# A Mamba-style mixer step: decay exponents from broadcast running sums instead of matmuls, and x and B transposed into banks 4 and 5

## The chip, the cores and the metric

The kernel runs on one core of a Trainium2 chip (trn2). The metric is the device time of one execution in microseconds. Three runs of the kernel before took 2757.2, 2757.87 and 2758.27 us; the median is 2757.87.

## What is computed

One decoder layer over 2048 tokens of 1024 channels, behind 16 learned meta tokens, all in fp32:

```python
hn = rms_norm(h, norm_mix_w);  proj = hn @ w_in            # u | z | xBC | dt
y  = concat(pool_mixer(u), ssd_mixer(z, xBC, dt))          # 512 + 1536 channels
h  = h + y @ w_out
h  = h + relu(rms_norm(h, norm_ffn_w) @ w_ff1)**2 @ w_ff2
out = rms_norm(h, norm_f_w)
```

The change is in the SSD mixer. It works in chunks of 128 tokens, on 4 groups of 6 heads. With `a_cs` the running sum of dt times a over a chunk:

```python
seg    = a_cs[l] - a_cs[s]                       # exponent, l: reading token, s: source token
decay  = exp(where(l >= s, seg, -inf))
y_diag = ((C[l] . B[s]) * decay) @ (x * dt)
```

`a` is negative, so the exponent is at most 0 wherever l >= s.

## The kernel before, in words

The 2048 tokens are worked in 4 blocks of 512, each of 4 chunks. Every large fp32 product is made of three products of rounded parts (high x high, high x low, low x high). A block goes through "items": a group's five conv units (B, C and three tiles of x) and its z (three units in block 0, four pieces by chunk in blocks 1 to 3), then four pool items, then 16 units of the output product. A unit is 24 matmuls of 128x512 (`up_unit`, L1692), a z piece 24 of 128x384 (L1716), and the output product L1736. In block 0 the weights are split on the way: ScalarE makes the high part (`high_part`, L500), GpSimd the low part (`low_part`, L508), SyncE stores both to DRAM (L705), and the later blocks load them back. ScalarE's high part of item N waits for the store of item N-2, since both use the same slot. After the four blocks the feed-forward part follows (L1996, L2028), which the change doesn't touch.

The mixer has 16 steps a block (`mixer_plan`): step q is group g, chunk c. The order on each engine is written out by hand. On TensorE a step is: `unit(n1)` (none in the last four steps), `slot3(q-1)`, `slot1(q)`, one to three units n2, `y_offset(q)`, `y_transposes(q-1)`. So the mixer's small matmuls stand between units of the next group, which cover what the other engines do in the meantime; the last four steps have one pool unit each.

`slot1` makes the exponents of 6 heads x 128 columns with matmuls: L1783 multiplies `seg_s` (selectors and the negated running sums of the group) with `seg_l` (running sums spread over the heads, and the head selectors), two matmuls of 128x384 into banks 4 and 5; in block 0 L1778 first puts -1e30 below the diagonal. It then transposes x and B (L1794) into bank 2 and, in block 0, z (L1803) into bank 3, and makes C.B in bank 3 (L1805). Bank 2 is used for the transposes of y too (`y_transposes`, L1817), which is why `slot1` waits for `yT_lo`, the low part of y (`y_low`, L2271). `slot3` is the product inside the chunk (L1829) and the new state (L1836); `y_offset` (L1811) reads the state.

ScalarE, in each step: evacuates n1 (`evac`), applies tanh, makes E from the exponents (block 0: one Exp, L1379; later: Relu with scale -1 from PSUM, L1382, and Exp, L1385, which clamps in place of the mask), spreads the negated sums once a group (L1318, L1322), copies x (L1394) and z (L1399), squares y (L1313), scales y by its root (`y_norm`, L1306, root on GpSimd, L983 and L984), evacuates n2, and takes the high part of y (`y_high`, L1299). VectorE: `y_finish` (the sum L2243 and the y product with the gate, L2245), the conv taps (`taps`, L2165), the state sum (L2262), the triangle mask on C.B (L2345, not in block 0), E times C.B (L2347), x times dt (L2351, L2353), `finish` of items (L2195, or the pool chain L2202 to L2219 for pool items), yo (L2363), and `y_low`.

The running totals of a block: softplus on VectorE (`softplus_rest`, L455 to L465, in three parts at items 2, 3 and 4), the totals by two matmuls (`running_totals`, L1841 and L1843: inside unit 7 in block 0, after item 6 later), copies by VectorE at the last item (L2312 to L2315), transposes of the totals on TensorE (L1904).

Of the kernel before, what the change touches and what calls it, by code (L numbers as in the profile page):

```python
# [6 lines left out]
P = 128  # L7
# [7 lines left out]
FAR = -1e30  # L15
# [6 lines left out]
TB = 512  # L22
# [138 lines left out]
def build(nc, x, meta, norm_mix_w, w_in, pool_w, pool_scale, conv_w, conv_b, dt_bias, a_log,  # L161
          d_skip, ssm_norm_w, w_out, norm_ffn_w, w_ff1, w_ff2, norm_f_w, out):
    ctx = ExitStack()
    with ctx:
# [49 lines left out]
        ident_r = sb("ident_r", [P, P], F32R)  # L214
        barred = sb("barred", [P, P], F32R)
# [4 lines left out]
        acsT = win_tmp[0:56, 0:TB].bitcast(F32R)  # L220
        head_of = sb("head_of", [56, 8])
        in_group = sb("in_group", [56, 4])
        not_group = sb("not_group", [56, 4])
        seg_l = sb("seg_l", [120, CH, HEADS_PER_GROUP, P], F32R)
        seg_s = sb("seg_s", [120, 2, TB], F32R)
# [5 lines left out]
        v, nv, ev, s_, q_, dA, acs, alast = [steps_of[:, i * NB:(i + 1) * NB] for i in range(8)]  # L231
# [48 lines left out]
        hn_scr = nc.dram_tensor("hn_scr", [3, 2, P, 4, TB], F32).ap()  # L280
        T_scr = nc.dram_tensor("T_scr", [2, 4, 7, P, 4, TB], F32).ap()
# [61 lines left out]
        acsT_hi_ready = sig("acsT_hi_ready", 1)  # L343
        acsT_lo_ready = sig("acsT_lo_ready", 1)
        seg_l_ready = sig("seg_l_ready", CH)
        seg_s_ready = sig("seg_s_ready", GROUPS)
        xb_ps = sig("xb_ps", STEPS)
        ab_ps = sig("ab_ps", STEPS)
# [3 lines left out]
        fall_ready = sig("fall_ready", STEPS)  # L352
        zs_ready = sig("zs_ready", STEPS)
# [51 lines left out]
        p_x = [sem(f"p_x{t}") for t in range(CH)]  # L405
# [4 lines left out]
        pick = acc[0:56, 0, 0:HEADS]  # L410
# [14 lines left out]
        below = F[:, 5956:6084]  # L425
# [218 lines left out]
        with nc.Block() as block:  # L644

            @block.sync
            def _(sp):
# [40 lines left out]
                initial = [s for s in signals if s.start and s not in (state_ready, up_out)]  # L688
# [258 lines left out]
            def _(pool):  # L947
# [8 lines left out]
                pool.affine_select(out=below[:, :], in_=ones[:, :], compare_op=ALU.is_gt,  # L956
                                   fill=0.0, base=0, pattern=[[-1, P]], channel_multiplier=1)
# [206 lines left out]
            def _(act):  # L1164
# [152 lines left out]
                def negated_sums(b, g):  # L1317
                    nc.scalar.activation(seg_s[0:56, g % 2, :],  # L1318
                                         ones[0:56, :].unsqueeze(1).to_broadcast([56, CH, P]),
                                         ACT.Copy, scale=in_group[:, g:g + 1])  # L1320
                    acsT_lo_ready.wait(act, b, 1)
                    nc.scalar.activation(seg_s[64:120, g % 2, :], acsT[:, :].bitcast(F32), ACT.Copy,  # L1322
                                         scale=not_group[:, g:g + 1]
                                         ).then_inc(seg_s_ready.sem, 1)

# [10 lines left out]
                for b in range(BLOCKS):  # L1336
# [7 lines left out]
                    for n in range(ITEMS_G if b else UNITS_G):  # L1344
# [11 lines left out]
                        if n == (ITEMS_G if b else UNITS_G) - 1:  # L1356
# [4 lines left out]
                                                 ).then_inc(gains_ready.sem, 1)  # L1361
                    pending = None
                    for q, g, c, n1, n2 in mixer_plan(b):
                        if q == 0:
                            acsT_ps.wait(act, b, 1)
                            nc.scalar.activation(acsT[0:HEADS, :], bank[3][0:HEADS, :], ACT.Copy
                                                 ).then_inc(acsT_hi_ready.sem, 1)
# [1213 lines left out]
```

## Time and profile before

| what | value |
|---|---|
| median of 3 runs | 2757.87 us |
| the profiled execution | 2759.15 us, its span 2757.4 us |
| TensorE busy | 2733.2 us, 99% |
| VectorE, ScalarE, GpSimd busy | 58%, 43%, 40% |
| DMA | 505.75 MB, 183 GB/s in the mean |
| mean granted TensorE clock | 0.998 |

The span runs from the first to the last instruction; the time of the execution also holds what lies around it. "Busy" on TensorE counts the modelled, overlapping spans of matmuls: one of 128x512 is shown with some 390 ns, while 24 in a row take 5.47 us. What a matmul costs on the path is therefore read from the chain of waits, not from its own duration.

### The profile page before, as it was taken

What the parts mean: (1) busy time and instruction counts of PE and PEld (TensorE: products, weight loads), DVE (VectorE), ACT (ScalarE), POOL (GpSimd) and SP (SyncE); (2) the same over time, 40 slices, a digit from 0 to 9 for tenths busy, and PEclk for the clock granted to TensorE, in tenths of its full rate; (3) what the DMA queues carried; (4) which work ended last, traced back from release to release, by engine and by line L of the source; (5) the groups of instructions that cost most, each with busy time, mean ns of one, the idle gap of its engine ahead of it and who ended that gap; (6) DMA issues with size and microseconds to landing.
All of it is one profiled execution on the core that took longest, in us unless ns stands there. A gap on an engine that the chain in (4) does not pass through costs nothing.

```text
span 2757.4 us, 37228 instructions
## 1 busy us (share of the span) xinstructions
PE 2733.2 (99%) x14110; PEld 2260.5 (82%) x14110; DVE 1604.2 (58%) x2236; ACT 1182.4 (43%) x2110; POOL 1096.3 (40%) x799
## 2 busy tenths in 40 slices
PE   8999999999999999999999999999999999999998
PEld 6788778888788887888888888888888888888887
DVE  4687623666426665157663466664445666666666
ACT  2465544455325554155542645555445322222223
POOL 1365541223101222003223587855555435353434
PEclk9999999999999999999999999999999999999999
DMA  9766486443556335554336446674444942333323
GB/s 291 243 220 200 154 294 240 183 170 137 185 196 229 123 134 189 198 211 170 138 134 248 172 158 240 221 279 168 148 146 163 352 153 92 135 125 129 123 92 153
DMA packets 215792, 505.75 MB, mean 183 GB/s; under 512 B 12970, under 2 KB 96558, under 8 KB 206142
## 3 DMA queue, kind: packets, MB, share of 16 engines
q1 hardware_dynamic: 215614, 503.37, 50.7%
q8 instruction: 113, 1.85, 0.3%
q14 instruction: 65, 0.53, 0.1%
HBM read 357.57 MB, written 145.75 MB: 183 GB/s over the span
## 4 chain that ended last, share of the span: by engine, by line
PE 95%; DVE 1%; DMA 1%; issue 1%; SPq 1%; POOL 0%; ACT 0%; DVEq 0%; ACTq 0%; POOLq 0%
PE bank L2028 22%; PE bank L1996 21%; PE bank L1692 21%; PE bank L1736 13%; PE bank L1716 7%; PE bank L1829 2%; PE bank L1836 2%; PE bank L1811 1%; PE bank L1794 1%; PE bank L1633 1%; PE bank L1783 1%; PE bank L1817 1%; PE bank L1805 1%; PE bank L1755 1%; PE bank L1951 0%
## 5 line engine op out<-in xcount | busy, mean ns | idle before, releaser
L1692 PE MATMUL bank<-hnT_hi,w_ring 128*128 128x512 f32 x1152 | 374.6, 396 | 0.0
L2165 DVE SCALAR_TENSOR_TENSOR acc<-pre,par,acc 128x512 f32<-128x512 f32 x240 | 216.9, 904 | 108.1 <-ACT pre L1230 102.4
L2028 PE MATMUL bank<-w_first,T_hi 128*128 128x512 f32 x896 | 275.9, 389 | 0.7 <-issue 0.7
L1692 PEld LDWEIGHTS bank<-hnT_hi,w_ring 128*128 128x128 f32 x1152 | 216.4, 188 | 44.9 <-ACT win_tmp L1339 0.5
L1996 PE MATMUL bank<-T_hi,w_both 128*128 128x512 f32 x768 | 242.1, 389 | 0.2 <-DVE ff L2448 0.2
L1736 PE MATMUL bank<-w_ring,T_hi 128*128 128x512 f32 x768 | 241.9, 396 | 0.0
L2507 DVE TENSOR_TENSOR acc_th<-bank,acc_th 128x512 f32<-128x512 f32 x224 | 150.0, 686 | 155.9 <-PE bank L2028 155.7
L983 POOL TENSOR_TENSOR small<-small 128x1 f32<-128x1 f32 (+1 forms) x71 | 20.5, 289 | 517.1 <-ACT yo L1313 311.1
L1692 PE MATMUL bank<-hnT_lo,w_ring 128*128 128x512 f32 x576 | 224.5, 390 | 0.0
L1716 PE MATMUL bank<-w_ring,hnT_hi 128*128 128x384 f32 x768 | 198.2, 338 | 0.0
L2028 PEld LDWEIGHTS bank<-w_first,T_hi 128*128 128x128 f32 x896 | 168.1, 188 | 35.9 <-issue 1.1
L508 POOL TENSOR_TENSOR w_both<-raw,w_both 128x1024 fp32r<-128x1024 f32 x52 | 126.1, 2427 | 176.1 <-ACT w_both L500 176.1
L1692 PE MATMUL bank<-hnT_hi,w_both 128*128 128x512 f32 x576 | 187.9, 398 | 0.7 <-ACT acc L1234 0.5
L1996 PE MATMUL bank<-b,w_both 128*128 128x512 f32 x768 | 179.5, 389 | 0.1
L2028 PE MATMUL bank<-w_first,T_lo 128*128 128x512 f32 x448 | 174.3, 389 | 0.0
L2028 PE MATMUL bank<-T_hi 128*128 128x512 f32 x448 | 174.3, 389 | 0.0
L2028 PE MATMUL bank<-T_lo,T_hi 128*128 128x512 f32 x448 | 174.3, 389 | 0.0
L2028 PE MATMUL bank<-T_hi,T_lo 128*128 128x512 f32 x448 | 174.3, 389 | 0.0
L1996 PEld LDWEIGHTS bank<-T_hi,w_both 128*128 128x128 f32 x768 | 144.2, 188 | 30.6 <-DVE ff L2448 0.6
L1736 PEld LDWEIGHTS bank<-w_ring,T_hi 128*128 128x128 f32 x768 | 142.8, 188 | 31.9 <-issue 2.9
L1996 PEld LDWEIGHTS bank<-b,w_both 128*128 128x128 f32 x768 | 144.0, 188 | 30.3 <-DVE ff L2440 0.5
L1996 PE MATMUL bank<-hnT_hi,w_both 128*128 128x512 f32 x512 | 163.3, 390 | 0.3 <-POOL w_both L1087 0.3
(310 smaller groups left out, 6264.1 us busy)
## 6 DMA issues: line engine op xcount, KB each, us to landing
w_ring<-w_scr SPq DMA_DIRECT2D x312, 512.0 KB, 4.2
T_scr<-stage SPq DMA_DIRECT2D x32, 1792.0 KB, 6.7
w_scr<-w_both SPq DMA_DIRECT2D x104, 512.0 KB, 4.0
pair_raw<-in_w_ff SPq DMA_DIRECT2D x36, 1024.0 KB, 5.5
third<-T_scr SPq DMA_DIRECT2D x28, 1024.0 KB, 4.8
pair_raw<-T_scr SPq DMA_DIRECT2D x28, 1024.0 KB, 4.8
raw<-in_w_in SPq DMA_DIRECT2D x36, 512.0 KB, 5.4
w_raw<-in_w_ff SPq DMA_DIRECT2D x12, 1024.0 KB, 7.5
```

Of the source, the lines that this page charges most:

```text
L508: nc.gpsimd.tensor_tensor(w_lo[:, N % 2, :], raw[:, N % RING, :], w_hi[:, N % 2, :].bitcast(F32), ALU.subtract).then_inc(w_lo_ready, 1)
L1633: mm = nc.tensor.matmul(m_bank(m)[0:16, (m % 4) * P:(m % 4 + 1) * P], m_hT[:, k, :], meta_w[m // 2 % 4][:, k, m % 2 * P:(m % 2 + 1) * P], ...
L1692: mm = nc.tensor.matmul(bank[s][:, :], w[:, k, :], t[:, k, :], start=(k == 0 and j == 0), stop=(k == KT - 1 and j == 2))
L1716: mm = nc.tensor.matmul(bank[s][:, 0:GW].rearrange("p (u c) -> p u c", c=P), t[:, k, tok], w[:, k, :, :], start=(k == 0 and j == 0), stop= ...
L1736: mm = nc.tensor.matmul(bank[4 + t][:, :], a, w[:, kk, :], start=(u == 0 and kk == 0 and j == 0), stop=(u == 7 and kk == 1 and j == 2))
L1755: mm = nc.tensor.transpose(dst[:, t * P:(t + 1) * P], h[:, t, k * P:(k + 1) * P], ident[:, :])
L1829: mm = nc.tensor.matmul(bank[6][rows, r * HEAD:(r + 1) * HEAD], E[:, r, rows], xdt[:, r * HEAD:(r + 1) * HEAD], start=True, stop=True, til ...
L1836: nc.tensor.matmul(bank[7][:, 0:GW], xb[:, GW:GW + P], xw[:, :], start=True, stop=True).then_inc(state_ps.sem, 1)
L1996: mm = nc.tensor.matmul(bank1(p, m), w[:, k, :], t[:, k, :], start=(m not in (2, 7, 3) and k == 0 and j == 0), stop=(m not in (1, 6, 5) an ...
L2028: mm = nc.tensor.matmul(bank[4 * half + t][:, :], a[:, k, tok], w[:, k, :], start=(SECOND[q % 7] not in GOES_ON and k == 0 and j == 0), st ...
L2165: ins = nc.vector.scalar_tensor_tensor(acc[:, s, 0:TB], pre[:, s, k:k + TB], w, acc[:, s, 0:TB], ALU.mult, ALU.add)
L2507: ins = nc.vector.tensor_tensor(dst, src, dst, ALU.add)
```

## The change

The matmuls of the exponents are left out, and with them `seg_l`, `seg_s`, the selectors and the mask below the diagonal. In their place the transposed running sums (24 rows x 512) are stored to DRAM by four DMAs, and for each step one DMA brings the 6 x 128 sums of its heads back, broadcast to all 128 partitions (384 KB; 16 loads a block, `load_sums`). From these, ScalarE makes the negated, clamped exponents of heads 0 to 2 by three Relus with a bias, VectorE the clamped exponents of heads 3 to 5 by three operations (`differences`), and ScalarE applies two Exps. The triangle mask on C.B is applied in block 0 too. x and B are transposed into banks 4 and 5 in turn, so `slot1` waits for the copy of x two steps back, and the wait for `yT_lo` moves to `y_transposes`. Running totals are made after item 5 in every block, their transposes after item 6; softplus is done by item 3.

```diff
-        seg_l = sb("seg_l", [120, CH, HEADS_PER_GROUP, P], F32R)
-        seg_s = sb("seg_s", [120, 2, TB], F32R)
+        sums = sb("sums", [P, CH, HEADS_PER_GROUP, P])
+        acs = sb("acs", [P, NB])
...
+                def store_sums(b):
+                    acsT_ready.wait(sp, b, 1)
+                    for g in range(GROUPS):
+                        rows = slice(g * HEADS_PER_GROUP, (g + 1) * HEADS_PER_GROUP)
+                        sp.dma_start(sums_scr[b, g].rearrange("c (r l) -> r c l", l=P),
+                                     acsT[rows, :].rearrange("r (c l) -> r c l", l=P)
+                                     ).then_inc(sums_stored.sem, 16)
+                def load_sums(b, g, c):
+                    if g:
+                        exp_ready.wait(sp, b, (g - 1) * CH + c + 1)
+                    sp.dma_start(sums[:, c, :, :].rearrange("p r l -> p (r l)"),
+                                 sums_scr[b, g, c].partition_broadcast(P)
+                                 ).then_inc(sums_loaded[c].sem, 16)
...
                         load(N0 + n, in_unit(n))
+                        if n == (8 if b else 10):
+                            store_sums(b)
+                        if n == (8 if b else 11):
+                            sums_stored.wait(sp, b, 16 * GROUPS)
+                            for c in range(CH):
+                                load_sums(b, 0, c)
+                        g, j = divmod(n, UNITS_G)
+                        if g >= 2 or g == 1 and j >= 5:
+                            after = {5: 0, 7: 1, (0 if b else 1): 2, 3: 3}.get(j)
+                            done = g if j >= 5 else g - 1
+                            if after is not None and 0 < done < GROUPS:
+                                load_sums(b, done, after)
...
-                        if n == (ITEMS_G if b else UNITS_G) - 1:
+                        if n == 6:
                             acs_ready.wait(act, b, 1)
...
+                            acsT_ps.wait(act, b, 1)
+                            nc.scalar.activation(acsT, bank[3][0:HEADS, :], ACT.Copy
+                                                 ).then_inc(acsT_ready.sem, 1)
...
-                        ab_ps.wait(act, b, q + 1)
+                        sums_loaded[c].wait(act, b, 16 * (g + 1))
                         ydiag_ps.wait(act, b, q)
-                        halves = E[:, :, :].rearrange("p (j r) l -> p j (r l)", j=2)
...
+                        for r in range(3):
+                            o = c * HEADS + g * HEADS_PER_GROUP + r
+                            fall = nc.scalar.activation(E[:, r, :], sums[:, c, r, :], ACT.Relu,
+                                                        scale=-1.0, bias=acs[:, o:o + 1])
+                        fall.then_inc(fall_ready.sem, 1)
+                        rise_ready.wait(act, b, q + 1)
+                        nc.scalar.activation(E[:, 3:6, :], E[:, 3:6, :], ACT.Exp)
+                        fall_ready.wait(act, b, q + 1)
+                        nc.scalar.activation(E[:, 0:3, :], E[:, 0:3, :], ACT.Exp, scale=-1.0
+                                             ).then_inc(exp_ready.sem, 1)
...
-                    for j in range(2):
-                        mm = nc.tensor.matmul(
-                            bank[4 + j][:, 0:GW].rearrange("p (r l) -> p r l", l=P),
-                            seg_s[:, g % 2, cols], seg_l[:, c, 3 * j:3 * j + 3, :],
-                            start=b > 0, stop=True)
-                    mm.then_inc(ab_ps.sem, 1)
...
-                    xb_ready.wait(pe, b, q)
-                    if q:
-                        yT_lo.wait(pe, b, q - 1)
+                    xb_ready.wait(pe, b, q - 1 if q else 0)
                     for i, j in enumerate((2, 3, 4, 0)):
-                        mm = nc.tensor.transpose(bank[2][:, i * P:(i + 1) * P],
+                        mm = nc.tensor.transpose(bank[4 + q % 2][:, i * P:(i + 1) * P],
...
                 def y_transposes(b, q):
                     yn_ready.wait(pe, b, q + 1)
+                    yT_lo.wait(pe, b, q)
...
-                        if b and n == 6:
-                            hT_ready.wait(pe, b - 1, KT - 1)
+                        if n == 5:
+                            if b:
+                                hT_ready.wait(pe, b - 1, KT - 1)
                             running_totals(b)
-                        if n == (ITEMS_G if b else UNITS_G) - 1:
+                        if n == 6:
                             acs_ready.wait(pe, b, 1)
...
+                def differences(b, q, g, c):
+                    sums_loaded[c].wait(dve, b, 16 * (g + 1))
+                    ydiag_ps.wait(dve, b, q)
+                    for r in range(3, HEADS_PER_GROUP):
+                        o = c * HEADS + g * HEADS_PER_GROUP + r
+                        rise = nc.vector.tensor_scalar(E[:, r, :], sums[:, c, r, :],
+                                                       acs[:, o:o + 1], 0.0, ALU.subtract, ALU.min)
+                    rise.then_inc(rise_ready.sem, 1)
...
                         if q:
                             y_finish(b, q - 1)
+                        differences(b, q, g, c)
                         taps(b, n1)
...
-                        if b:
-                            steps.link(nc.vector.tensor_tensor(cb, cb, tri[:, :], ALU.mult))
+                        steps.link(nc.vector.tensor_tensor(cb, cb, tri[:, :], ALU.mult))
```

## Rows read from the trace of the kernel before

**Rows 1.** The page: span, busy time of the engines, chain by engine.
```profile
span 2757.4 us, 37228 instructions
...
PE 2733.2 (99%) x14110; PEld 2260.5 (82%) x14110; DVE 1604.2 (58%) x2236; ACT 1182.4 (43%) x2110; POOL 1096.3 (40%) x799
...
PE 95%; DVE 1%; DMA 1%; issue 1%; SPq 1%; POOL 0%; ACT 0%; DVEq 0%; ACTq 0%; POOLq 0%
```
**Rows 2.** Chain of waits through a step of block 0: start us, us, what.
```profile
262.94 0.34 PE bank L1778 x2
263.28 0.36 PE bank L1783 x2
...
270.75 0.33 PE bank L1817 x3
```
**Rows 3.** Chain of waits, a step of block 1.
```profile
574.67 0.35 PE bank L1783 x2
```
**Rows 4.** Timeline of TensorE, 300 to 310 us: start, us, line, operation, [idle before <-releaser].
```profile
305.88 1.04 PE L1794 MATMUL bank<-ident,F 128*128 128x128 f32 x4 [1.77 <-DVE T_lo L2271]
```
**Rows 5.** Windows behind it: us, TensorE busy (instructions), granted clock, DMA share, GB/s.
```profile
306.00:309.00 3.00, 3.00 (x12) 0.50 1.01 328
309.00:312.00 3.00, 3.00 (x14) 0.94 0.27 98
```
**Rows 6.** Groups by line and shape: xcount | busy us, mean ns | idle before.
```profile
L2058 DVE TENSOR_SCALAR barred<-F 128x128 fp32r<-128x128 f32 x1 | 0.2, 213 | 0.0
...
L2271 DVE SCALAR_TENSOR_TENSOR T_lo<-bank,par,T_hi 128x128 fp32r<-128x128 f32 x192 | 55.3, 342 | 48.5 <-ACT T_hi L1299 48.5
...
L1299 ACT ACTIVATE T_hi<-bank,par 128x128 fp32r<-128x128 f32 x192 | 56.8, 375 | 19.4 <-PE bank L1817 19.1
...
L1385 ACT ACTIVATE E<-E 128x768 f32<-128x768 f32 x48 | 40.7, 847 | 1.5
...
L2245 DVE TENSOR_TENSOR y<-y,zs 128x384 f32<-128x384 f32 x16 | 28.2, 1762 | 0.6
```
**Rows 7.** Timeline of VectorE: the y product in four steps (blocks 0, 0, 1, 1).
```profile
262.95 2.31 DVE L2245 TENSOR_TENSOR y<-y,zs 128x384 f32<-128x384 f32 x1
...
331.42 0.56 DVE L2245 TENSOR_TENSOR y<-y,zs 128x384 f32<-128x384 f32 x1
...
693.47 0.56 DVE L2245 TENSOR_TENSOR y<-y,F 128x384 f32<-128x384 f32 x1
...
703.46 0.56 DVE L2245 TENSOR_TENSOR y<-y,F 128x384 f32<-128x384 f32 x1
```
**Rows 8.** Chain of waits: the transposes of y in the last steps of blocks 0 and 1.
```profile
335.01 0.33 PE bank L1817 x3
...
697.99 0.33 PE bank L1817 x3
...
707.24 0.33 PE bank L1817 x3
```
**Rows 9.** Timelines of VectorE and TensorE at the start of block 0.
```profile
104.83 1.12 DVE L455 SCALAR_TENSOR_TENSOR E<-E 128x96 f32<-128x96 f32 x4
...
106.42 0.50 PE L1692 MATMUL bank<-hnT_hi,w_both 128*128 128x512 f32 x1 [0.24 <-ACT pre L1230]
...
112.64 0.50 PE L1692 MATMUL bank<-hnT_hi,w_both 128*128 128x512 f32 x1 [0.47 <-ACT acc L1234]
...
117.73 0.26 DVE L2315 TENSOR_TENSOR dte<-E 128x96 f32<-128x96 f32 x1
```
**Rows 10.** ScalarE's wait; DMA 104 to 144 us; store landings; DMA 484 to 516 us.
```profile
133.61 1.06 ACT L500 ACTIVATE w_both<-raw 128x1024 fp32r<-128x1024 f32 x1 [2.40 <-DMA w_scr<-w_both]
...
DMA packets 8939, 11.95 MB, mean 299 GB/s; under 512 B 319, under 2 KB 6843, under 8 KB 8937
...
DMA to landing us min/median/max: 2.6/4.0/10.6
...
GB/s 0 0 0 0 0 0 0 0 0 0 0 0 0 0 0 61 333 374 399 292 389 410 369 297 236 210 292 584 343 410 512 389 389 343 440 405 415 420 420 420
```

More of the change, by code:

```diff
@@ L230, in build @@
         steps_of = E.rearrange("p r l -> p (r l)")
-        v, nv, ev, s_, q_, dA, acs, alast = [steps_of[:, i * NB:(i + 1) * NB] for i in range(8)]
+        v, nv, ev, s_, q_, dA, alast = [steps_of[:, i * NB:(i + 1) * NB] for i in range(7)]
+        acs = sb("acs", [P, NB])
         dtt = sb("dtt", [P, NB])
@@ L342, in build @@
         acsT_ps = sig("acsT_ps", 1)
[L343 to L346, printed above, removed]
+        acsT_ready = sig("acsT_ready", 1)
+        sums_stored = sig("sums_stored", 16 * GROUPS, 0)
+        sums_loaded = [sig(f"x_then_sums_loaded{c}", 16 * GROUPS, 16)
+                       for c in range(CH)]
         xb_ps = sig("xb_ps", STEPS)
-        ab_ps = sig("ab_ps", STEPS)
         zc_ps = sig("zc_ps", STEPS)
@@ L404, in build @@
         p_sumsq, p_xn = sem("p_sumsq"), sem("p_xn")
-        p_x = [sem(f"p_x{t}") for t in range(CH)]
+        p_x = [s.sem for s in sums_loaded]
         p_ps, p_hi, p_lo = sem("p_ps"), sem("p_hi"), sem("p_lo")
         win = w_in[0]
-        pick = acc[0:56, 0, 0:HEADS]
         m_in = F[0:16, 0:1024]
@@ L687, in _ @@
                 x_tile(3)
-                initial = [s for s in signals if s.start and s not in (state_ready, up_out)]
+                initial = [s for s in signals if s.start and s not in (state_ready, up_out, *sums_loaded)]
                 for j in range(5, 12):
@@ L1361, in _ @@
                                                  ).then_inc(gains_ready.sem, 1)
+                            acsT_ps.wait(act, b, 1)
+                            nc.scalar.activation(acsT, bank[3][0:HEADS, :], ACT.Copy
+                                                 ).then_inc(acsT_ready.sem, 1)
                     pending = None
                     for q, g, c, n1, n2 in mixer_plan(b):
[L1364 to L1367, printed above, removed]
-                            negated_sums(b, 0)
                         if n1 is not None:
@@ L1393, in _ @@
                         xw_ready.wait(act, b, q)
-                        nc.scalar.activation(xb[:, :], bank[2][:, :], ACT.Copy
+                        nc.scalar.activation(xb[:, :], bank[4 + q % 2][:, :], ACT.Copy
                                              ).then_inc(xb_ready.sem, 1)
@@ L1870, in _ @@
                             continue
-                        if b == 0 and n == 7:
-                            unit(b, n, 0, 4)
-                            running_totals(b)
-                            up_unit(unit_of(b, n), n % 2, 4, KT)
-                        else:
-                            unit(b, n)
+                        unit(b, n)
                         if b == 0 and n in (1, 2):
@@ L1923, in after_mixer @@
                         if t == 0:
-                            exponent_read(b, STEPS)
+                            xb_ready.wait(pe, b, STEPS)
                         elif t == 2:
```

90 lines of the change are left out of this document (9 added, 81 removed).

## The prediction

> **What bounds the kernel.** I read the page first. TensorE is busy for 2733.2 of 2757.4 us and the chain that ended last is 95% TensorE [rows 1]: a microsecond of matmul that goes is a microsecond of time, unless a wait takes its place. So the other views are for two questions: what the removed matmuls cost on that chain, and how much slack the other engines have at the places where TensorE asks for their results. The profiled execution took 2759.15 us, 1.75 us around its span; the median of the three runs shown, 2757.87, is 1.28 us lower. I make the sum on the trace and apply the difference to the median.
>
> **Removed matmuls.** In the chain through block 0 each of 16 steps holds two matmuls of L1778 (0.34 us) and two of L1783 (0.36): 0.70 us, 11.2 in all [rows 2]. Blocks 1 to 3 have only L1783, 0.35 us in each of 48 steps: 16.8 [rows 3]. Together 28.0 us; nothing covers them and nothing of the change puts work on TensorE in their place (transposes, products and running totals stay, only moved).
>
> **A stall that goes.** At the start of the last group of block 0 TensorE waits 1.77 us for the low part of y (T_lo, L2271), because x and B are transposed into bank 2, which y uses too [rows 4]. With banks 4 and 5 that wait moves to the transposes of y, one step later, where it is long done. The idle time was paid twice: behind it the granted clock was 0.50, so the 1.2 GHz level, for 3 us, and 0.94 for the next 3 [rows 5]: half of 3 and 0.06 of 3 are 1.7 us. Gain 3.5 us. What is late next is y scaled by its root: about 0.9 us lost again. Net -2.6.
>
> **The new chain of a step.** Old: matmuls, clamp and Exp on ScalarE, copy of x, squares, root on GpSimd, scaling of y, transposes of y. New: y product on VectorE, then three subtractions with a clamp, then two Exps of 384 on ScalarE, and the rest. ScalarE used to do Exp before it needed VectorE; now it waits behind the y product. The prices: a subtraction reads SBUF with a pointer scalar, 128x128; the trace has one TENSOR_SCALAR of this size, 213 ns, while a low part from PSUM of the same size takes 342 ns. I take the first, as it is the same operation (some 0.5 us for three, since starts overlap ends), and keep 0.9 as the upper bound. A 128x128 Relu with a bias I price as L1299, 375 ns, 1.1 us for three; they run while VectorE still works on y, so they cost nothing; without this cover they would add 1.1. The Exps replace L1385 of 768 (847 ns); two halves at 0.4 to 0.5 are 0.85 [rows 6].
>
> In the main steps of block 0 the y product ends at 265.26 [rows 7]. Then 0.45 subtractions, 0.85 Exps, 0.5 copy of x, 0.4 copy of z, 0.6 squares, 0.95 root, 0.6 scaling: 269.65. The transposes of y came at 270.75 [rows 2] and are now due 0.70 earlier, 270.05: no wait, by 0.4 us. VectorE gets 0.5 and, in block 0, 0.3 for the triangle mask per step; it sat idle over 1 us there, and its y product waits for GpSimd anyway. Cost 0, bounds 0 and +3 (0.5 in six steps). In blocks 1 to 3 each main step has over 2 us left.
>
> In the last four steps of a block there is one unit of matmuls and no cover. For blocks 1 to 3, step 14: product to 694.03 [rows 7], plus 0.45, 0.85, 0.5, 0.65, 0.95 and 0.6 is 698.1; due 697.99 - 0.35 = 697.64 [rows 8]; a wait of 0.45. Step 15: 704.02 gives 708.1, due 706.89: 1.2 us. Three blocks: 5.0 us. The cause is the pool item, which VectorE finishes ahead of the y product. In block 0 the same step: 331.98 [rows 7] plus 4.5 (a z copy more) is 336.5, due 335.01 - 0.70 = 334.3 [rows 8]: 2.2 us, and 1.7 for the clock, as it is longer than the idle time of rows 4. Its two neighbours, whose y product waits for GpSimd instead, lose 0.3 each by the same steps. Together 4.5. Whether 1.2 us of idle time lowers the clock no row shows: bounds 0 and +5.1 (three times 1.7).
>
> **The start of block 0.** Running totals move from item 7 to item 5, and TensorE waits for them in line. In the trace four polynomial steps take 1.12 us and end at 105.95; six more at 0.28 end at 107.6, while TensorE is free at 106.2 [rows 9]: 1.4 us. Then it waits behind item 6 until VectorE has copied the totals. VectorE comes there 1.1 us later than now; the difference of L2315, two SBUF inputs, starts about when GpSimd begins a low part of 2.4 us. By the y product, 1762 ns in the mean beside the low parts of block 0 [rows 6] and 0.56 elsewhere [rows 7], it is held until 117.6. Item 7 then starts near 118.3 instead of 112.64 [rows 9]; less 0.8 us of work moved out, 4.9 us. If the difference slips in ahead of GpSimd it is 2.5. Two idle stretches of 1.4 us and more: 2.7 us for the clock (bounds 0 and 3.4).
> SyncE is in order too. The four stores of the sums stand before the store of item 7's weights, which used to go out some 10 us earlier and now waits for the sums, to about 120.6. Behind it come 1.5 MB of weights, 1.57 MB of broadcast sums, and the 2 MB of h. In this stretch the queue moved 299 GB/s in the mean with short pauses, and ScalarE already waited 2.4 us for such a store [rows 10]. At an estimated 340 GB/s while busy (299 over a share of 0.88), the store of item 9 lands near 144.5, and item 11 needs it split: a wait of 1.8 us (bounds 0 and 7). Start in all: +9.4, bounds 2 and 15.
> In blocks 1 to 3 the sums are ready some 7 us before the next weight loads are due, in 12 us without a packet [rows 10]: 0. The 12 later loads per block wait for an Exp ahead of weight loads that have three units of slack: 0. The DVE setup that goes was done while TensorE multiplied: 0.
>
> **Sum.** -28.0 -2.6 +0 +5.0 +4.5 +9.4 = -11.7 us: 2747.3 for the profiled execution, 2746 for the median.
>
> **A rule against the change.** The y product beside low parts is three times as long as elsewhere [rows 6, 7]. The subtractions come right behind it, when GpSimd has just finished, so I let them run free.
> The Trainium skill (SBUF — State Buffer, section Who interferes with whom) says that tensor_scalar in a two-port mode and GpSimd shut each other out completely, whoever issued first keeping the ports. By that rule, the trace's y product agrees, and the subtractions are exposed as well; it is the fourth rival.
>
> **Rivals.**
> 1. The waits don't arise (the difference slips through, transfers land in time, the chain is shorter than counted): -28.0 - 2.6 + about 2 is -28.6, 2729. For it: all the idle time before TensorE is 24 us here, most of it before 40 us. Against: the tails have under 2 us of slack and get 2 to 3 us more chain. 0.20.
> 2. The y chain becomes the bound: subtractions 0.9 instead of 0.5, six waits in the main steps of block 0 (+3), 0.4 in each of nine tail steps (+3.6), and the clock falls at the 1.2 us waits (+5.1). Total -11.7 + 11.7 = 0, 2758: no change. 0.15.
> 3. Slower: weight stores in block 0. Each of 12 loads of sums holds SyncE for an Exp, and the store behind it is needed 14.9 us after its unit. At 4.0 us to landing [rows 10] there is slack of 4 us. The longest such landing is 10.6 us (the store that ScalarE waited for); if all behaved so, 2.2 us each is 26. It decides from a landing of 8.4 us on. With it -11.7 + 26 = +14: 2772. For it only the 2.4 us wait of rows 10; against, the 2 MB load in front of that store comes once a block. 0.05.
> 4. The port: a subtraction issued just after a low part began waits 2.4 us. It decides if VectorE arrives earlier than the low part ends; in 16 steps with 0.4 us of slack this is 32 us, -11.7 + 32 = +20: 2778. Against: the y product stands in front and takes that wait itself. 0.03.
> That the change doesn't do what it says is no case: the matmuls are gone from the program.
>
> **How the numbers follow.** Forecast 0.57. A measurement can tell about 0.2% here, 5.5 us: faster means under 2752.4. The forecast gives 0.56 faster and 0.01 same, rival 1 is faster, rival 2 same but for 0.02 on either side, rivals 3 and 4 slower: 0.78, 0.12, 0.10. The range 2731 to 2756 leaves out rivals 3 and 4, the half of rival 1 that gains over 27 us, and the tip of rival 2: just under 2 in 10.
>
> **What would show it.** L1778 and L1783 absent; the chain through a main step 0.70 and 0.35 us shorter; TensorE waits before the transposes of y in the last two steps of each block; a wait near 106 and one near 114 us in block 0; no wait for T_lo at 304 and no clock of 0.50 there. I am wrong if the tails have no waits (rival 1), if they have them in main steps (rival 2), or if ScalarE's w_both copies wait for DMA beyond 150 us (rival 3).

## The result and the profile after

The changed kernel takes 2767.2 us in the median of 7 runs (2766.4 to 2770.5), the kernel before on the same chip 2758.3 (2756.9 to 2759.8). The ratio is 1.0034, with a 95% interval of 1.0024 to 1.0043. That is 9 us slower, where 12 us faster was forecast. The profiled execution has a span of 2768.8 us against 2757.4: +11.4. It was the slowest of the seven, 3.3 us above their median, so what is added up below from its trace is somewhat dearer than the usual execution.

The page of the changed kernel: span, engines, chain by engine, landings of two kinds of load (calls, KB each, median us from issue to landing).

```profile
span 2768.8 us, 37377 instructions
...
PE 2712.4 (98%) x13950; PEld 2234.2 (81%) x13950; DVE 1622.1 (59%) x2413; ACT 1183.7 (43%) x2286; POOL 1084.4 (39%) x798
...
PE 88%; DVE 4%; issue 2%; ACT 2%; DMA 1%; POOL 1%; SPq 1%; DVEq 0%; ACTq 0%; POOLq 0%
...
sums<-sums_scr SPq DMA_DIRECT2D x64, 384.0 KB, 5.0
raw<-in_w_in SPq DMA_DIRECT2D x36, 512.0 KB, 6.9
```

Against [rows 1], TensorE has 160 matmuls fewer and is busy 20.8 us less. 28.0 us were removed, so about 7 came back; matmuls at a lower clock account for most of it, as the windows below show. Its idle time rose from 24.2 to 56.4 us, by 32.2, and -20.8 + 32.2 = +11.4. The chain is 88% TensorE where it was 95%: VectorE and ScalarE hold the rest.

The removal itself is as told. The chain of waits of the changed kernel, through a main step of block 0:

```profile
242.71 0.85 PE bank L1815 x24
243.56 0.84 PE bank L1822 x2
244.40 0.44 PE bank L1779 x4
244.84 0.33 PE bank L1788 x3
```

The exponent matmuls, which stood between L1822 and L1779 [rows 2], are gone. A step that took 15.32 us (255.43 to 270.75 us, from transposes of y to transposes of y) takes 14.60 (177.75 to 192.35).

The waits of the changed kernel's TensorE: line, what ended the wait, us in total, times, longest.

```profile
PE bank L1803 <- ACT y L1327: 12.0, 11, 2.3
PE bank L1822 <- DVE yo L2321: 7.0, 2, 4.1
...
PE bank L1886 <- DVE dte L2279: 3.8, 1, 3.8
PE bank L1796 <- DVE S L2217: 3.4, 1, 3.4
PE bank L1700 <- POOL w_both L502: 3.0, 2, 1.6
PE bank L1827 <- DVE E L459: 1.5, 1, 1.5
```

None of these stood in the trace of before, whose only wait over 1 us behind the first 40 us, for T_lo [rows 4], is gone. I cut the program at the last transposes of y in block 0, which start at 367.6 us in the kernel before and at 385.0 in the changed one. Block 0 with the start lost 17.4 us; the rest of the program (2389.8 us before, 2383.8 after) gained 6.0. The next three views are of the changed kernel's timeline. First, TensorE's rows with the idle time before them:

```profile
119.28 0.61 PE L1886 MATMUL bank<-ident,acs 128*24 128x128 f32 x4 [3.76 <-DVE dte L2279]
...
315.04 1.36 PE L1822 MATMUL bank<-xw,xb 128*128 128x384 f32 x2 [2.86 <-DVE yo L2321]
...
346.48 0.55 PE L1803 MATMUL bank<-ident,y 128*128 128x128 f32 x3 [2.25 <-ACT y L1327]
...
362.55 1.65 PE L1822 MATMUL bank<-xw,xb 128*128 128x384 f32 x2 [4.10 <-DVE yo L2321]
...
712.12 0.55 PE L1803 MATMUL bank<-ident,y 128*128 128x128 f32 x3 [1.16 <-ACT y L1327]
722.70 0.55 PE L1803 MATMUL bank<-ident,y 128*128 128x128 f32 x3 [1.58 <-ACT y L1327]
```

What VectorE did ahead of three of them:

```profile
116.97 2.26 DVE L2279 TENSOR_TENSOR dte<-E,acs 128x96 f32<-128x96 f32 x1
...
311.08 3.44 DVE L2159 SCALAR_TENSOR_TENSOR F<-pre,acc 128x512 f32<-128x512 f32 x2
314.45 0.54 DVE L2321 TENSOR_TENSOR yo<-bank,ea 128x384 f32<-128x384 f32 x1
...
357.76 2.82 DVE L2180 TENSOR_TENSOR acc<-pre 128x527 f32<-128x527 f32 x1
...
361.95 0.55 DVE L2321 TENSOR_TENSOR yo<-bank,ea 128x384 f32<-128x384 f32 x1
```

And GpSimd's low parts beside them:

```profile
116.77 2.34 POOL L502 TENSOR_TENSOR w_both<-raw,w_both 128x1024 fp32r<-128x1024 f32 x1 [4.60 <-ACT w_both L494]
...
311.40 2.57 POOL L502 TENSOR_TENSOR w_both<-raw,w_both 128x1024 fp32r<-128x1024 f32 x1 [0.66 <-ACT w_both L494]
...
357.67 2.35 POOL L502 TENSOR_TENSOR w_both<-raw,w_both 128x1024 fp32r<-128x1024 f32 x1 [0.65 <-ACT w_both L494]
```

The pattern is the same three times. A VectorE operation from SBUF is held until a low part ends (the pool item's first sum takes 2.82 us, 0.71 elsewhere), and what TensorE needs stands behind it in VectorE's order. Twice that is yo, for which the state product (L1822) waits; at 116.97 it is the difference of the totals itself, as forecast. Step 15 in the kernel before, VectorE, GpSimd and TensorE:

```profile
343.75 0.71 DVE L2216 TENSOR_TENSOR acc<-pre 128x527 f32<-128x527 f32 x1
...
345.83 0.55 DVE L2363 TENSOR_TENSOR yo<-bank,ea 128x384 f32<-128x384 f32 x1
...
345.80 2.37 POOL L508 TENSOR_TENSOR w_both<-raw,w_both 128x1024 fp32r<-128x1024 f32 x1 [2.32 <-ACT w_both L500]
...
346.43 0.91 PE L1836 MATMUL bank<-xw,xb 128*128 128x384 f32 x2
```

There yo was through 0.05 us before TensorE came for it. The hold is only a part of the new waits: 2.1 of the 4.10 us, and 2.2 of the 2.86 (3.44 for two operations that take 1.28 without a low part). The other 2.0 of the 4.10 is the order itself. Before the change TensorE came for yo 3.6 us behind the end of xw (342.79); now it is itself waiting for xw, comes for yo 1.0 us behind it (357.42 and 358.45), and the pool item still stands between the two.

ScalarE, meanwhile, waits for the stores of weights:

```profile
128.08 1.06 ACT L494 ACTIVATE w_both<-raw 128x1024 fp32r<-128x1024 f32 x1 [7.57 <-DMA w_scr<-w_both]
...
136.87 1.06 ACT L494 ACTIVATE w_both<-raw 128x1024 fp32r<-128x1024 f32 x1 [6.76 <-DMA w_scr<-w_both]
```

Two more follow, to 146.83 and 152.10 us (3.22 and 2.90). Between 100 and 160 us the trace of before has one such wait, of 2.40 us [rows 10]. SyncE's queue in the changed kernel shows where they come from, the stores of the sums and then that of item 7's weights, which in the kernel before was issued at 110.35 us:

```profile
120.53 1.32 SPq L728 DMA_DIRECT2D sums_scr<-win_tmp  x4
121.90 0.82 SPq L699 DMA_DIRECT2D w_scr<-w_both  x2
```

The clock, by windows (us, TensorE busy, weight loads, VectorE, ScalarE, GpSimd, granted clock, DMA share, GB/s):

```profile
155.00:175.00 20.00, 16.60 (x86) 12.62 (x85) 19.61 (x28) 12.63 (x32) 10.25 (x8) 0.83 0.60 198
312.00:320.00 8.00, 5.14 (x25) 4.07 (x21) 6.54 (x12) 4.21 (x12) 4.13 (x3) 0.79 0.86 304
...
362.00:370.00 8.00, 7.45 (x24) 5.67 (x25) 6.75 (x17) 1.99 (x6) 2.88 (x4) 0.71 1.01 375
722.00:725.00 3.00, 2.30 (x30) 1.77 (x31) 0.86 (x5) 1.98 (x5) 2.58 (x3) 1.00 0.97 358
725.00:728.00 3.00, 3.00 (x15) 2.46 (x14) 2.86 (x8) 0.62 (x2) 1.06 (x2) 1.00 0.98 366
```

The first three cost 20 x 0.17 + 8 x 0.21 + 8 x 0.29 = 7.4 us. The 7 us of the balance are net of the 1.7 that the kernel before lost behind T_lo, so these windows leave some 1.5 us of it without a place. Behind the waits of 1.56 to 1.58 us in blocks 1 to 3 the clock did not fall.

### The profile page after: what moved, and what is told of

Same layout as the page of the kernel before. It is cut to its first block, busy times and chain, and to the rows that moved or that the text cites. A ratio compares the mean times of both kernels' runs of the same rounds, so it can differ in the third digit from the quotient of the medians.

```text
span 2768.8 us, 37377 instructions
## 1 busy us (share of the span) xinstructions
PE 2712.4 (98%) x13950; PEld 2234.2 (81%) x13950; DVE 1622.1 (59%) x2413; ACT 1183.7 (43%) x2286; POOL 1084.4 (39%) x798
## 4 chain that ended last, share of the span: by engine, by line
PE 88%; DVE 4%; issue 2%; ACT 2%; DMA 1%; POOL 1%; SPq 1%; DVEq 0%; ACTq 0%; POOLq 0%
PE bank L2010 22%; PE bank L1978 21%; PE bank L1700 16%; PE bank L1744 13%; PE bank L1724 7%; PE bank L1822 1%; PE bank L1815 1%; PE bank L1641 1%; PE bank L1796 1%; DVE acc L2129 1%; PE bank L1803 1%; PE bank L1779 1%; PE bank L1763 1%; PE bank L1933 0%; DMA meta_w<-in_w_in 0%
```

## The experiments

I had two questions. In the start of block 0: is it the order of SyncE's queue, the bytes, or the held difference? In the tails (the last four steps of a block): is it the order on ScalarE, or GpSimd's low parts? Every run but the last two has three rounds beside the kernel before, whose median was 2758.2 to 2759.3 each time. "Block 0" is the start of its last transposes of y, and "rest" is the span less that, both in the profiled execution; since that can lie some us off the median, gains are taken from the medians. Code is shown shortened.

**1. The sums' stores behind the store of item 7's weights.**
```
-  if n == (8 if b else 10): store_sums(b)
-  if n == (8 if b else 11): ... load_sums(b, 0, c)
+  if n == (8 if b else 11): store_sums(b)
+  if n == (8 if b else 12): ... load_sums(b, 0, c)
```


> Edit: in block 0 alone SyncE issues the four stores of the sums, and the first four broadcast loads behind them, one weight load later, so that the store of item 7's weights goes out ahead of the wait for the sums. Theory A (the order of SyncE's queue makes the start dear): in the changed kernel ScalarE waited 7.57 and 6.76 us for stores of weights, and TensorE 1.06, 1.34 and 1.64 us for what lies behind. With the store sent near 112 us the 7.57 goes to under 1, and TensorE's waits at 132.30 and 140.51 us go; with the clock behind them 3 to 6 us: about 2762. Theory B (the bytes of the broadcasts and of h crowd the transfers, whatever their order): the ScalarE waits only move, sum above 10 us, and the time stays within 1 us of 2767. The waits at 119.28 us (3.76), 315.04 (2.86) and 362.55 (4.10) stay by both.

Measured 2761.6, 5.6 us less than the changed kernel; block 0 ends at 376.5 instead of 385.0, the rest is 2383.7. The store of item 7's weights is issued at 110.75 us instead of 121.90. Between 119 and 154 us TensorE has no wait left, and the 3.40 for the state's sum is gone too:

```profile
117.83 1.03 PE L1886 MATMUL bank<-ident,acs 128*24 128x128 f32 x4 [3.77 <-DVE dte L2279]
154.13 0.55 PE L1803 MATMUL bank<-ident,y 128*128 128x128 f32 x3 [0.28 <-ACT y L1327]
```

Theory A holds for the time and for the places. One point of it missed: ScalarE still sat idle 7.24 us before that high part, but now what ended the wait was TensorE, which still read from the slot that the part overwrites. How long ScalarE sat idle was not the measure; what ended its wait was.

**2. The load of h later.** `if n == 12` becomes `if n == (12 if b else 28)`.


> Edit: in block 0 alone the load of h (2 MB) is issued 16 weight loads later, near the middle of the block, where the queue has pauses. Theory A (order): ScalarE's 7.57 us wait stays, as that store stands ahead of h; the waits of 3.22 and 2.90 near 147 and 152 us shrink, TensorE gains the 1.64 at 150.52 at most and perhaps some of the 3.40 at 159.61: 1 to 3 us. Theory B (bytes): the queue is relieved of 2 of some 5 MB between 121 and 150 us, and the waits of 6.76, 3.22 and 2.90 go to under 2 in all: 4 to 6 us, about 2762.

2763.9, 3.3 us less; block 0 380.6. The waits at 132 to 150 us shrink from 4.04 to 0.38 and 0.94, the one for the state's sum from 3.40 to 1.90, but a new one of 1.33 for yo comes at 146.86. By the time this lies between the two theories: bytes seem to count as well, and less than order. It is near the edge of what the runs can tell (2762.8 to 2767.3, against 2766.4 to 2770.5). These waits also differ between executions: in runs 3 and 4, which leave SyncE's order and its loads as they are, those between 120 and 160 us add to 6.2 and 4.9 us, against 7.4 in the changed kernel's trace.

**3. Squares of y ahead of the Exps**, on ScalarE, all blocks.
```
+  if q: y_squares(b, q - 1)
   rise_ready.wait(act, b, q + 1)
   (Exps, copies of x and z)
-  if q: y_squares(b, q - 1)
```


> Edit: on ScalarE the squares of y stand ahead of the two Exps of a step instead of behind the copies of x and z; they then run while VectorE does its three subtractions, and GpSimd's root beside the Exps. Theory A (the tails are a chain of latency through ScalarE): the scaling of y comes about 1.2 us earlier, so the waits of 1.16 and 1.58 us in the last two steps of blocks 1 to 3 fall to under 0.4 each (about 7 us in all), that of 2.25 at 346.48 to about 1: 7 to 10 us with the clock, about 2759. Rival: the Exps come later by the squares, 0.6 us, the masked product and the diagonal products with them, and VectorE's later work moves: the waits change their name (G of L2305 in the place of y) and less than 3 us is gained.

2752.4: 14.8 us less than the changed kernel and faster than before (ratio 0.9975, 0.9966 to 0.9984). The rest goes from 2383.8 to 2377.0, so the tails of blocks 1 to 3 gave 6.8, as theory A said; in place of 1.16 and 1.58 there is one wait of 0.79 per block, before L1815. Block 0 gave 9.9. That is more than I expected, because most of the waits for yo went as well (0.47 us of them is left): the scaling, so the high part, so the low part came at other times relative to VectorE's work. One low part came at a bad time. Waits of TensorE, then VectorE and GpSimd in step 14 of this run:

```profile
PE bank L1815 <- issue: 6.3, 5, 3.4
...
PE bank L1803 <- ACT y L1327: 0.3, 1, 0.3
```

```profile
338.41 2.70 DVE L2311 TENSOR_TENSOR xw<-xb,dte 128x384 f32<-128x384 f32 x1
...
338.29 2.40 POOL L502 TENSOR_TENSOR w_both<-raw,w_both 128x1024 fp32r<-128x1024 f32 x1 [1.06 <-ACT w_both L494]
```

The low part began 0.12 us ahead of xw, which then took 2.70 instead of 0.55 us, and L1815 waited 3.40. The profile names no releaser for this wait; `slot3` waits for xw ahead of L1815, and xw ended at 341.11, 0.10 us before L1815 began.

**4. yo ahead of the finishes**, in steps 11 and 15 of block 0: the wait for the offset product and yo stand before `finish(b, held ...)` and `finish(b, n1)`.


> Edit: in block 0's steps 11 and 15 VectorE's product yo (0.55 us) stands ahead of the finishes of items and the pool item, which GpSimd's low part holds up. Theory A (TensorE's state product waits for yo, and yo only for what stands before it on VectorE): the waits of 2.86 us at 315.04 and 4.10 us at 362.55 go to under 0.5, and the clock that was 0.79, 0.81 and 0.71 behind them returns to 1.0: 7 to 9 us, about 2759. Rival (the port holds whatever VectorE issues there, and the finish that now comes later holds ScalarE's evacuations instead): yo itself takes 2.3 us or more, or the wait moves to the next step's y; less than 3 us.

2770.1 (2767.7 to 2772.7): nothing gained, and the 2.9 us more are not clear of the noise. yo came in time, and the two waits changed their name and grew:

```profile
315.45 0.87 PE L1788 MATMUL bank<-ident,F 128*128 128x128 f32 x3 [3.63 <-DVE F L2159]
...
367.90 1.22 PE L1744 MATMUL bank<-w_both,T_hi 128*128 128x512 f32 x2 [5.15 <-DVE y L2209]
```

Theory A falls in the form in which I put it. TensorE waits for whichever result stands behind the held operation; changing the order around it moved the wait.

**5. A signal of their own for the totals**, given by the copy to acs and no longer by dte two operations behind it; ScalarE copies the transposed sums ahead of its Exps.


> Edit: the running totals get a signal of their own as soon as they are copied, so that TensorE's transposes wait for that and not for the difference dte that stands third behind it, and ScalarE copies the transposed sums ahead of its three Exps. Theory A (GpSimd's low part holds the difference L2279 for 2.26 us instead of 0.26, and all of the sums' way, TensorE included, stands behind it): TensorE's wait of 3.76 us falls by 2.5 to 3, the stores of the sums go out 3 us earlier, and the waits for weights at 132.30, 140.51 and 150.52 (4.04 in all) shrink by 1 to 3: 4 to 6 us, about 2762. Rival (the whole wait is VectorE coming late, behind two finishes; or the start is bound by the transfers whatever the sums do): the wait only turns into one for weights, under 2 us gained.

2765.4, against 2759.3 for the kernel before in that set: 6.1 more than before where the changed kernel had 8.9, so 2.8 gained, which is not clear of the noise (2762.7 to 2769.4). The profiled execution, 7.8 us below that of the changed kernel, was the fastest of its ten, and the changed kernel's was the slowest of its seven. The wait of 3.76 fell to 1.19, by the 2.6 of theory A, but 0.85, 1.62 and 1.17 for weights and what hangs on them and 3.37 for the state's sum stayed. It is between the two.

**6. Edits 1, 2, 3 and 5 together.**


> Edit: four edits of single runs together: the sums' stores one load later, h sixteen loads later, squares of y ahead of the Exps, the totals' own signal. Apart, the first three gained 5.6, 3.3 and 14.8 us on the changed kernel. Theory A (the start, through transfers, and the tails, through ScalarE, are separate losses; store order and h are partly the same loss): the tails' 15 remain whole and the start gives 8 to 12 (of 25 us of waits and clock there): 2740 to 2744, and the remaining waits are 3.40 before L1815 near 330 us and the totals'. Rival (one limit of transfers under all of the start): squares plus the better of the others, about 2747.

2742.7 (2741.6 to 2744.3): 24.5 us less than the changed kernel, and the ratio to the kernel before is 0.9940 (0.9924 to 0.9956). It is as good as the best version I found and beats both kernels. Block 0 ends at 365.2, the rest is 2375.3. What is left of waits over 1 us between 100 and 2700 us is 1.54 and 1.18 for the totals, then 1.94, 1.03 and

```profile
331.17 1.55 PE L1816 MATMUL bank<-xdt,E 128*64 128x64 f32 x24 [3.40 <-issue]
```

with a granted clock of 0.50 from 331 to 334 us and 0.51 from 334 to 337.

**7, 8. The high part later in the tail of block 0**, on top of 6. In 7 it comes behind y_high in all four last steps (1.4 us later), in 8 behind the evacuation in step 14 alone (0.5 us later).


> Edit: the four edits, and in the last four steps of block 0 ScalarE's high part of the next weights comes behind the high part of y instead of ahead of the evacuation. Theory A (in the run with the squares ahead, the scaling of y came earlier, so the high part, so GpSimd's low part, which then held VectorE's product xw for 2.70 instead of 0.55 us, and TensorE waited 3.40 for it): the low part starts 1.4 us later, behind xw; the wait of 3.40 goes, with its clock 3 to 5 us less than the run with four edits. Rival (the low part now holds the next SBUF operation, the y product, instead): the wait turns up one step later, no difference.

> Edit: the kernel with four edits, and in step 14 of block 0 alone ScalarE's high part comes behind the evacuation (0.5 us later) instead of ahead of it. With all four tail steps moved by 1.4 us the time rose from 2742.7 to 2749.9 us, so the low part then met other operands. Theory A (it is a matter of what VectorE issues next when GpSimd begins: at 331 us the low part began 0.12 us ahead of the product xw): with 0.5 us of delay xw is through first, the wait of 3.40 us before L1815 goes, and nothing else in reach is held, since the next operation from SBUF is the y product more than 2.4 us later: 3 to 5 us less than with four edits, 2738 to 2740. Rival (moving the low part only moves the wait, as before): 2742 or more.

2749.9 and 2746.2: 7.2 and 3.5 us more than with four edits. In both, xw is through and the 3.40 is gone (1.26 stays). In 7 there are 1.99 for yo and 2.94 for y instead. Both have a wait for the state's sum in the middle of the block besides (1.57 and 1.74 us near 284 us). In 8 there is 4.00 for yo in the next step, whose timeline of VectorE and GpSimd is

```profile
332.03 0.55 DVE L2326 TENSOR_TENSOR yo<-bank,ea 128x384 f32<-128x384 f32 x1
...
342.30 2.71 DVE L2179 TENSOR_TENSOR F<-acc 128x512 f32<-128x512 f32 x1
```

```profile
331.93 2.41 POOL L503 TENSOR_TENSOR w_both<-raw,w_both 128x1024 fp32r<-128x1024 f32 x1 [1.55 <-ACT w_both L495]
...
341.72 2.74 POOL L503 TENSOR_TENSOR w_both<-raw,w_both 128x1024 fp32r<-128x1024 f32 x1 [2.22 <-ACT w_both L495]
```

The rival was right twice. In 8 the next low part moved as well and now met the pool item, which one had held in the changed kernel too. The first pair of rows shows what isn't held: yo, with one operand in PSUM, ran its 0.55 us inside a low part.

**9. The state's sum ahead of the taps in steps 1 and 2**, on top of 8.


> Edit: the former, and in steps 1 and 2 VectorE adds the state ahead of the taps of the next item (2.3 us), which stood in front. Theory A (the waits of 3.40 us at 159.61 in the changed kernel and of 1.94 us with four edits come from the state's sum standing behind y, subtractions and taps): that wait goes, 2 to 3 us less than the former. Rival (the taps are as urgent: the tanh of that item, ScalarE's next evacuation and TensorE's next unit wait for them): the wait turns up at a unit of weights or at L1789, under 1 us.

2743.7, 2.5 less than 8. The waits of 0.23 and 1.94 for the sum are gone, and 1.22 and 0.94 for the scaling of y stand in their place, so both theories had half of it, and the waits of the start add to 2.2 us in both runs. What the trace of 9 has less is the wait of 1.74 us at 284.82, where two taps beside a low part had taken 3.99 us, and a fall of the clock (0.60 and 0.83 from 164 to 170 us in 8). Run 6, without this edit, has neither of them. So the gain is not shown to come from the edit. The wait for yo in step 15 (3.99) is as it was.

**10, 11. Two controls on the kernel before**: the late load of h, and the squares ahead of the Exps.


> Control, the kernel before with the late load of h alone. If the start of the kernel before was not bound by transfers (its trace has no wait of TensorE between 100 and 170 us for weights), it is the same within 1 us: the 3.3 us which this gave on the changed kernel are then a loss of the change and not an old one. If the transfers bound it too, 2 us or more.

> Control, the kernel before with the squares of y ahead of its Exps. There the exponents came from TensorE, and the Exps did not need VectorE. By theory A (the order of ScalarE was right for the old chain and wrong for the new) it gains nothing and may lose up to 3 us, since the Exps now wait for the y product. If it gains 5 us or more, the gain of 14.8 on the changed kernel had little to do with the change.

2757.9 (ratio 1.0000, 0.9990 to 1.0009) and 2766.5 (1.0030, 1.0020 to 1.0040). Both went by theory A, the second further than it said: 8 us slower. In its trace TensorE waits 4.2 us in all before the product inside the chunk (L1829) and 2.9 for yo. The start of the kernel before was not bound by transfers, and the order that gains 15 us with the new chain loses 8 with the old one.

**12. Four edits and the state's sum**, five rounds.


> Edit: the four edits and the state's sum ahead of the taps in steps 1 and 2, without moving the high part. It gained 2.5 us beside the moved high part. Theory A (start and tail of block 0 add up): 2742.7 - 2.5 = 2740, the wait of 3.40 us before L1815 near 330 us unchanged, the last step without its wait of 4.0. Rival (a start that ends 2 us earlier shifts low parts and VectorE in the tail against each other): 2742 or more, with new waits after 300 us.

2743.0 (2741.7 to 2744.2): no gain on 6, as its rival said. The two waits for the sum are exchanged for 1.19 and 0.94, and one of 1.71 appears at 282.9 us, in the middle of the block, as in 7, 8 and 13 (1.57, 1.74 and 1.68) and not in 6 and 9.

**13. The last step emptied**, five rounds: 9, and in step 15 ScalarE's high part behind the evacuation, GpSimd's low part behind its two products.


> Edit: as the run with the state's sum ahead and the high part of step 14 behind the evacuation, and in step 15 too; and there GpSimd does its two products of the step before the low part, which held VectorE's pool item for 2.71 instead of 0.69 us and with it yo. Theory A (the port: what VectorE issues from SBUF inside a low part waits for its end, so an emptied spot has no wait): the pool item takes 0.7 again, the wait of 4.0 us before L1822 falls to under 1, and so 3 to 5 us are gained on 2743.7: 2739 to 2741. Rival (the low part of step 15 now ends 3 us later and holds the product y with the gate, or the weights come late for the down units): a wait before the first L1744 of 2 to 3 us, 2742 or more.

2743.2 (2741.0 to 2744.1). The pool item's sum took 0.69 us with the low part out of its way, so the low part is what had held it:

```profile
340.71 0.69 DVE L2181 TENSOR_TENSOR F<-acc 128x512 f32<-128x512 f32 x1
```

But TensorE still waited 1.99 us for yo, the part of the wait that is order and not hold; the product of y with the gate took 1.42, and TensorE waited 1.06 for it. Half a microsecond came of it (2743.7 to 2743.2), within what the runs can tell. Runs 6, 9, 12 and 13 are the same within 1 us, with the waits in different places.

## Why the prediction was wrong

Forecast for the profiled execution -11.7, measured +11.4: 23.1 us apart, 17.3 of them in block 0 (forecast +0.1, measured +17.4) and 5.8 behind it (forecast -16.8 + 5.0 = -11.8, measured -6.0).

- **Removed matmuls, -28.0: right.** Main steps are 0.72 us shorter in block 0 by the chain. With four edits the rest is 2375.3 against 2389.8 us, -14.5 with 3 x 0.79 of waits in it; -16.9 without them, for a forecast of -16.8. So close an agreement is partly luck: the six runs with the squares moved and the other three edits have rests from 2375.3 to 2378.2.
- **The stall for T_lo, -2.6: right in the wait**, which is gone, and what I put late next, y scaled, is late. The 1.7 us for the clock were a matter of that one execution: in the traces of runs 10 and 11, both of the kernel before with one edit each, the same wait of 1.77 us is followed by a granted clock of 1.00 from 306 to 309 us.
- **Main steps, 0: right**, but for two waits of 0.26 and 0.27 us in block 0.
- **Tails of blocks 1 to 3, +5.0: right in mechanism, too small.** The waits are 1.16 and 1.58 us, 8.2 in all. From the end of the y product (707.46) to the end of the scaling (712.07) it took 4.6 us, where I had 4.1: the subtractions take 0.59 instead of 0.45, and from the squares to the scaling, where the root is made, it is 1.45 instead of 0.95. GpSimd's two operations of the root now run beside xdt and xw (710.08 to 711.42) and take 1.34 us, where they took 0.82 in the kernel before (from 704.75). The clock bound of 0 was right.
- **Tail of block 0, +4.5: this step failed, and by most.** It measured 14.3 (3.25, 7.0 and 4.0). The waits for the scaling of y (0.62, 2.25 and 0.38) add to 3.25 where I had 2.8. But I followed only the chain through ScalarE to y, and never asked when yo would be there. In the kernel before, the pool item's sum of step 15 began 2 us ahead of the low part; in the changed one the low part began first, by 0.09 us. So the pool item was held, in step 11 a finish was, and yo behind them kept the state product waiting 2.86 and 4.10 us, 7.0 us that no term had. Some 4.3 of them are hold, and 2.7 are VectorE's order, since TensorE now comes for yo sooner behind xw; run 13, without a hold in step 15, keeps 1.99. The clock of 0.79 and 0.71 cost 4.0 where I had 1.7.
- **The start, "a wait of 1.8 us (bounds 0 and 7)": this term failed too.** The start measured 16.1 us (5.3, 7.4 and 3.4) for a forecast of 9.4, just over its bound of 15. The totals' part was right: two waits were forecast, one of 1.4 us and one behind item 6, and they came with 1.54 and 3.76, with the difference held beside the low part as said; 4.9 us were forecast for them and 5.3 measured. The waits for weights and what hangs on them were 1.06 + 1.34 + 1.64 and 3.40 for the state's sum behind them, 7.4 us, where I had 1.8. The clock lost 3.4 us (155 to 175 us) where I had 2.7, but that nearness is luck: I had put it behind the two waits for the totals, where it stayed at 1.00, and it came behind the wait for the state's sum. I had seen that SyncE waits for the sums ahead of item 7's store, and even when (120.6 us; it was 121.90), and then followed only the bytes behind it to the store of item 9. ScalarE's high part of item 9, which needs the slot of item 7, already waited 7.57 us for that first store. Run 1 shows that the place of the stores and first loads in the queue is worth 5.6 us, run 2 that h is worth some 3, run 10 that h cost nothing before the change.

These differences, 5.6 and 0.7 for the start's waits behind the totals and its clock, 7.0 and 2.3 for yo and the clock of the tail, 0.5 for the scaling of y, 0.4 for the totals and 0.5 for main steps, add to 17.0 of the 17.3 us of block 0. Of the 5.8 behind it 3.2 are the tails, 0.9 and 0.4 two single waits (at 520.51 and 1238.03 us), 0.7 a wait for a low part that grew from 0.28 to 1.02 (at 1862.48), and 0.6 stay unassigned.

- **Rivals.** The fourth was right about the resource and wrong about the operation. All 192 subtractions took 272 to 289 ns each, and none of block 0 overlapped a low part, so whether one would be held is not shown; the held operations were others, ahead of results that TensorE needed. The second was right about the y chain in the tails and wrong about main steps and the clock. The third did not occur as told, but the sign that I gave for it did by a hair: one w_both copy waited for DMA to 152.10 us. Behind that there is one such wait in block 0's weights, 4.60 us to 448.69, and the kernel before has it too (4.49 us to 431.21). The first, 2729, stayed out of reach: with four edits 2742.7.

What stays open: with four edits block 0 still ends 11 us later than 367.6 less the 13.8 us of matmuls and stall. The waits listed at run 6 with those of 0.2 to 0.6 us elsewhere in it are about 11, and the clock lost 3 more behind the 3.40; no version removed them all at once. Whether another placement of low parts could was not tried beyond runs 7, 8 and 13.

## What to carry over

When work moves from the engine that bounds to others that have time, the time doesn't come back by the sum of the engines' shares but by the places where the bound engine asks for results: write out for each of them what is queued ahead on the supplying engine, also for results that the change doesn't touch, such as yo here. A new dependence can turn an old order of issue wrong. Here the squares of y belonged behind the Exps in the old chain and ahead of them in the new one, and that one move was worth 15 us, more than the change was forecast to gain. And in a queue that is issued in order, a store that waits for late data holds back the ready one behind it, here from 110.35 to 121.90 us.

## What the runs showed of the hardware

**What a GpSimd low part holds.** While the 2.4 us subtraction of 128x1024 ran, a VectorE operation with all operands in SBUF that was issued after it took until its end: 2.26 us for a 128x96 difference that took 0.26 in the kernel before, 2.70 for xw (0.55 elsewhere), 2.82 and 2.71 for the pool item's sums (0.71 and 0.69), and 2.33 for a COPY of 128x16 in run 4 (0.17). With an operand in PSUM yo took its usual 0.55 inside one. The Trainium skill (SBUF — State Buffer, section Who interferes with whom) says that an instruction with two SBUF inputs contends with a GpSimd instruction that reads SBUF and one with a single SBUF input in the ordinary mode does not; this trace agrees, by the 2.26 and the 0.55 us.

**Idle time and the granted clock.** The same wait of TensorE in the same place was followed by either clock:

| wait | clock behind it |
|---|---|
| 1.77 us for T_lo, to 305.8 or 305.9 | 0.50 before [rows 5]; 1.00 in runs 10 and 11 (to 309) |
| 1.94 us for the state's sum, to 164.5 and 164.3 | 1.00 in run 6; 0.60 in run 8 (164 to 167) |
| 2.25 to 2.29 us for y scaled | 1.00 in the changed kernel and run 5; 0.58 and 0.57 over the next four us in runs 1 and 2 |
| 3.40 us before L1815, to 331.17 | 0.50 and 0.51 in run 6 (to 337) |

0.50 is the 1.2 GHz level. The waits of 1.56 to 1.58 us were followed by 1.00 in all three blocks. So the length of one idle stretch alone doesn't decide it here, and a single profile gives no fixed price for such a fall.
